# Regrouping TensorE's 512- and 256-column matmuls by width, and moving two operands by 32 bytes

## What is computed

```python
def conv_glu_ffn(x, norm_g, w_up, conv_w, conv_b, w_down):
    h = rms_norm(x, norm_g) @ w_up              # 1024 -> 2 * 2816
    c = conv_b + sum(conv_w[j] * shifted(h, j) for j in range(3))
    gate, up = jnp.split(c, 2, axis=-1)
    return x + (jax.nn.silu(gate) * up) @ w_down    # 2816 -> 1024

def swiglu_ffn(h, w13, w2):
    gate, up = jnp.split(h @ w13, 2, axis=-1)
    return (jax.nn.silu(gate) * up) @ w2

def reference(...):
    for layer in range(2):                      # phases L0 F0 L1 F1
        x = (diff_pool_layer, swa_layer)[layer](x, ...)
        x = conv_glu_ffn(x, ...)
    x = x + 0.5 * swiglu_ffn(rms_norm_2(x, g1), w13_1, w2_1)     # F2
    x = x + y @ w_out                           # y: conv module and attention of x (MIX)
    x = x + 0.5 * swiglu_ffn(rms_norm_2(x, g2), w13_2, w2_2)     # F3
    return rms_norm_2(x, final_norm)
```

## Time and profile before

| | |
|---|---|
| median of 3 runs | 1034.45 us (1033.99 to 1034.63) |
| the profiled execution | 1034.77 us |
| its span, first to last instruction | 1033.0 us |
| PE busy | 1008.0 us, 98% |
| PEld busy | 905.3 us, 88% |
| DVE / ACT / POOL busy | 746.7 / 625.5 / 354.9 us |
| mean granted TensorE clock | 0.998 |
| read from HBM | 181.4 MB, 177 GB/s over the span |

### The profile page before, as it was taken

One profiled execution on the slowest core, in us unless ns is written; L12 is line 12 of the kernel. 1 busy time (PEld: TensorE's weight loads), 2 busy tenths in 40 slices (PEclk: granted clock), 3 DMA queues, 4 the chain that ended last, 5 costly groups with the idle time before them and its releaser, 6 DMA issues.

```text
span 1033.0 us, 15900 instructions
## 1 busy us (share of the span) xinstructions
PE 1008.0 (98%) x6476; PEld 905.3 (88%) x6476; DVE 746.7 (72%) x1009; ACT 625.5 (61%) x880; POOL 354.9 (34%) x189
## 2 busy tenths in 40 slices
PE   7999999999998899999999999999999899999997
PEld 7889988888987798888888888888999698888886
DVE  5886999874577779998548765654799887666543
ACT  6776677663377477766436555544669866455531
POOL 1062176640000025675102545510148223555300
PEclk9999999999999999999999999999999999999999
DMA  9533575537441335656553755556342247555441
GB/s 351 207 135 123 214 270 209 201 131 257 146 163 42 125 142 209 239 188 207 180 200 123 247 202 175 191 204 220 123 155 95 83 172 259 180 204 186 141 163 41
DMA packets 27143, 183.45 MB, mean 178 GB/s; under 512 B 3008, under 2 KB 3136, under 8 KB 5824
## 3 DMA queue, kind: packets, MB, share of 16 engines
q1 hardware_dynamic: 26496, 181.40, 49.2%
q10 hardware_dynamic: 576, 1.05, 0.3%
HBM read 181.39 MB, written 1.05 MB: 177 GB/s over the span
## 4 chain that ended last, share of the span: by engine, by line
PE 85%; DVE 6%; ACT 5%; issue 2%; POOL 1%; DMA 0%; DVEq 0%; POOLq 0%; ACTq 0%
PE psum L335 85%; DVE wlo L1564 2%; ACT whi L1030 1%; POOL Y L2246 1%; ACT Pb L1165 1%; DVE Pb L1696 1%; DVE Pb L1567 1%; DVE QK L1570 0%; DVE QR L1564 0%; DMA gain_x<-in_x 0%; DVE bias L1570 0%; ACT Ob L1373 0%; ACT PT L1030 0%; ACT sq L1156 0%; DVE st L1567 0%
## 5 line engine op out<-in xcount | busy, mean ns | idle before, releaser
L335 PE MATMUL psum<-G,whi 128*128 128x512 f32 (+1 forms) x1856 | 551.3, 359 | 6.5 <-DVE wlo L1564 6.5
L1564 DVE TENSOR_TENSOR wlo<-raw,whi 128x2048 fp32r<-128x2048 f32 (+1 forms) x170 | 386.9, 2291 | 177.6 <-ACT whi L1030 177.5
L335 PE MATMUL psum<-G,wlo 128*128 128x256 f32 x1568 | 442.9, 282 | 0.0
L1030 ACT ACTIVATE whi<-raw 128x2048 fp32r<-128x2048 f32 (+1 forms) x170 | 315.9, 1869 | 148.0 <-PE psum L335 136.3
L335 PEld LDWEIGHTS psum<-G,whi 128*128 128x128 f32 x1856 | 330.6, 189 | 59.1 <-DVE G L1570 6.4
L335 PEld LDWEIGHTS psum<-G,wlo 128*128 128x128 f32 x1568 | 298.0, 190 | 0.1
L335 PE MATMUL psum<-A2room,whi 128*128 128x512 f32 (+1 forms) x784 | 228.6, 355 | 0.0
L2246 POOL TENSOR_TENSOR A2room<-Ab,A2room 128x512 fp32r<-128x512 f32 x44 | 146.8, 3337 | 127.6 <-ACT A2room L1030 127.6
L335 PE MATMUL psum<-A2room,wlo 128*128 128x256 f32 x656 | 184.9, 282 | 0.0
L335 PEld LDWEIGHTS psum<-A2room,whi 128*128 128x128 f32 x784 | 138.3, 188 | 20.6
L2246 POOL TENSOR_TENSOR Ab<-Cb 128x512 f32<-128x512 f32 x44 | 109.6, 2491 | 107.7 <-ACT Cb L1073 107.1
(11 more groups left out here) (192 smaller groups left out, 1034.7 us busy)
## 6 DMA issues: line engine op xcount, KB each, us to landing
raw<-in_wst SPq DMA_DIRECT2D x165, 1024.0 KB, 4.9
bias<-in_bias_c SPq DMA_DIRECT2D x1, 2048.0 KB, 9.3
raw<-in_wst SPq DMA_DIRECT2D x3, 512.0 KB, 8.0
raw<-in_wst ACTq DMA_DIRECT2D x4, 256.0 KB, 6.3
out<-bias SPq DMA_DIRECT2D x4, 256.0 KB, 2.1
gain_x<-in_x SPq DMA_DIRECT2D x3, 256.0 KB, 6.5
bias<-in_bias_a SPq DMA_DIRECT2D x1, 512.0 KB, 7.9
bias<-in_invcnt SPq DMA_DIRECT2D x1, 512.0 KB, 6.8
```

Of the source, the lines that this page charges most:

```text
L335: return pe.matmul(o, a, b, start=start, stop=stop, skip_group_check=True)
L1030: return act.activation(o, i, ACT.Copy)
L1564: return dve.tensor_tensor(o, a, b, op)
```

## The change

1. `wide` takes a list of tiles in place of a half, and issues for its two blocks of channels: all 512-column matmuls of the first block, all 256-column ones of the first, all 256-column ones of the second, all 512-column ones of the second. Most calls now cover the whole chunk (eight tiles); in F2 and F3 the first two chunks are still done in halves.
2. `down_wide` issues for an even bank two matmuls of 512 and then two of 256 columns, for an odd one two of 256 and then two of 512.
3. G2 is declared ahead of gain_x, so it starts at 128 modulo 256; gain_x does too, as before.
4. A2 starts at the beginning of its room in every phase, at 128 modulo 256. F3 keeps its place. Mhi and Mlo stay at 160.

```diff
+        G2 = sb("G2", [P, DT, 2, S], F32R)
         gain_x = sb("gain_x", [P, DT + DT * S])
         X = gain_x[:, DT:].rearrange("p (a b) -> p a b", a=DT)
-        G2 = sb("G2", [P, DT, 2, S], F32R)
...
-            A2 = A2room[:, 8:8 + FT * 2 * S].rearrange("p (t a s) -> p t a s", t=FT, a=2)
-            A2last = A2room[:, 0:FT * 2 * S].rearrange("p (t a s) -> p t a s", t=FT, a=2)
+            A2 = A2room[:, 0:FT * 2 * S].rearrange("p (t a s) -> p t a s", t=FT, a=2)
 
             def activations(ph):
-                a = A2last if ph == F3 else A2
-                return a[:, :, 0, :], a[:, :, 1, :]
+                return A2[:, :, 0, :], A2[:, :, 1, :]
...
-            def wide(b, i, h, ph=None, normed=None):
+            def wide(b, i, ks, ph=None, normed=None):
 
                 h3, l3 = weights(i, DT)
-                if h == 0:
+                if ks[0] == 0:
                     pe.wait_ge(s_lo, low_done(i))
-                for n in range(2):
-                    for k in range(4 * h, 4 * h + 4):
+
+                def highs(n):
+                    for k in ks:
                         if n == 0 and ph is not None:
                             pe.wait_ge(s_glo, 8 * ph + k + 1)
-                        if n == 0 and normed is not None:
+                        if n == 0 and normed is not None and k % 4 == 0:
                             pe.wait_ge(s_nlo, 2 * normed + k // 4 + 1)
-                        ws = slice(n * P, n * P + P)
-                        mm(bank[b + n], h3[:, k, ws], G2[:, k, :, :].rearrange("p a s -> p (a s)"), k == 0, False)
-                        last = mm(bank[b + n][:, 0:S], l3[:, k, ws], G2[:, k, 0, :], False, k == DT - 1)
-                if h == 1:
+                        last = mm(bank[b + n], h3[:, k, n * P:n * P + P], G2[:, k, :, :].rearrange("p a s -> p (a s)"),
+                                  k == 0 and n == 0, k == DT - 1 and n == 1)
+                    return last
+
+                def lows(n):
+                    for k in ks:
+                        mm(bank[b + n][:, 0:S], l3[:, k, n * P:n * P + P], G2[:, k, 0, :], k == 0 and n == 1,
+                           k == DT - 1 and n == 0)
+
+                highs(0)
+                lows(0)
+                lows(1)
+                last = highs(1)
+                if ks[-1] == DT - 1:
                     last.then_inc(s_used, 1)
...
-                    for kk in range(2):
-                        k = 2 * j + kk
-                        mm(o, h3[:, kk, ws], A2[:, k, :, :].rearrange("p a s -> p (a s)"), k == 0, False)
-                        done = mm(o[:, 0:S], l3[:, kk, ws], A2[:, k, 0, :], False, k == FT - 1)
+                    for high in ((True, False) if b % 2 == 0 else (False, True)):
+                        for kk in range(2):
+                            k = 2 * j + kk
+                            begin, end = k == 0 and high == (b % 2 == 0), k == FT - 1 and high == (b % 2 == 1)
+                            if high:
+                                done = mm(o, h3[:, kk, ws], A2[:, k, :, :].rearrange("p a s -> p (a s)"), begin, end)
+                            else:
+                                done = mm(o[:, 0:S], l3[:, kk, ws], A2[:, k, 0, :], begin, end)
...
-                        for h in range(2):
-                            wide(b, c0 + 2 * p + e, h, None, n if p == NARROW and e == 0 else None)
+                        wide(b, c0 + 2 * p + e, range(DT), None, n if p == NARROW and e == 0 else None)
...
-                    wide(at(ph, 4) + 2 * e, c0 + e, 0, ph if e == 0 else None)
+                    wide(at(ph, 4) + 2 * e, c0 + e, range(4), ph if e == 0 else None)
                 for e in range(2):
-                    wide(at(ph, 4) + 2 * e, c0 + e, 1, ph if e == 0 else None)
+                    wide(at(ph, 4) + 2 * e, c0 + e, range(4, DT), ph if e == 0 else None)
...
-                        wide(b + 2 * e, c0 + 2 * p + e, 0)
-                        wide(b + 2 * e, c0 + 2 * p + e, 1)
+                        wide(b + 2 * e, c0 + 2 * p + e, range(DT))
```

## The result

The changed kernel is slower: 1041.18 us median (1040.65 to 1041.71), against 1034.54 us for the kernel before in the same comparison; ratio 1.0065, 95% interval 1.0053 to 1.0078. The profiled execution took 1040.65 us with a span of 1038.9 us, 5.9 us more than before, so its trace holds nearly all of the difference. The forecast was 1029.2 us and the range 1024 to 1038; both missed.

What follows compares the result with a forecast made beforehand. TensorE, never waiting in wide stages, was taken as the bound. From the profiled 1034.77 us, regrouping took 5.25 and the move nothing, giving 1029.5; the median, 0.3 lower, was forecast at 1029.2 us, range 1024 to 1038.

Steps and rivals of the forecast that it cites:

- What bounds the kernel: Whole kernel: TensorE, busy 98%, waits for nobody in the seven wide stages; only distances between matmul starts count.
- What regrouping brings: Wide up and down projections: 3184 of 3616 width changes go, at 1.65 ns each, saving 5.25 us.
- price of a change of width: Wide stages: each switch between 512 and 256 columns costs 1.65 ns, from 346.7 against 343.4 ns a pair.
- The rule that spoke against it: Wide stages: the skill's gap, columns divided by clock plus 2.5 ns, makes regrouping worth 0 us.
- What the move brings: G2 and A2 moved 32 bytes to 128 modulo 256: 256-column matmuls assumed to stay at 116.6 ns, no gain or loss.
- slower rival: Both operands at 128 collide at 256 columns: wide lose 6.0 against 5.25 us gained, narrow up to 4.4; 1038 us, chance 0.18.
- the forecast's own test: F0's narrow stage, first A2room matmul to norm sum: 11.20 us if residue is neutral, 11.35 or more if it costs.
- narrow price: 1320 narrow matmuls with moving G or A2: up to 4.4 us lost, 1.3 if only 384 in A2room count.
- tokens-first chunks: 192 matmuls that also come to 128/128: could win 0.3 us, left out of the sum.
- Waits: Wide stages: no new wait costed; narrowest cover 0.25 us in F2's first half chunk; nothing added.
- No change: Rival: a low in a row costs 118.3 ns, or order is worth nothing; 1034.5 us, chance 0.15.
- more than forecast: Rival: same residue removes half the fixed 6.4 ns on 3128 matmuls, 10 us more; 1019 us, chance 0.13.

Runs made afterwards that it cites:

- order alone: The changed kernel with G2 and A2 put back at 160 modulo 256 (A2 of F3 at 128), regrouping kept; 1041.03 us, ratio to the kernel before 1.0061.
- two and two: F2's order, two highs then two lows, in a run of several orders with G2 64 bytes past the weights, edited from the changed kernel; 1031.78 us.
- grouped at 64: The changed kernel with wide moving operands 64 bytes past the weights and narrow inputs 32 past, grouped by width; 1032.56 us, ratio to the kernel before 0.9977.

## Why the prediction was wrong, point by point

**What bounds the kernel.** Right. PE waits for nobody in the wide stages after either, and all of the loss in the stage table's wide and narrow stages comes out of distances between matmuls.

**What regrouping brings.** This is the step that failed. It took 226.8 ns for highs from F3's down projection and 116.6 ns for lows from the narrow stages, and charged their difference to the alternation, 346.7 - 343.4 = 3.3 ns. But F3's row is at distance 0 and the narrow rows at distance 32. At 32 a high in a row takes 233.1 ns (order alone); at 0 a low takes 119.4 (changed kernel). No row of the trace of before shows both at one distance. F3's row has the weights moving besides: with the weights stationary, highs at distance 0 take 228.1 ns in runs of 16 and 232.5 in runs of four. The "price of a change of width" of 1.65 ns is not there where it could be tested: at distance 64 two and two is as fast as 16 and 16. In place of -5.25 us grouping at distance 32 brings +6.5. The prediction also called the narrow rows 116.6 "in two places, to 0.1 ns"; a third place in the same trace, F1's first narrow part, has 117.8. It named the risk in its last sentence, that no row shows a high in a row with weights stationary, but gave that risk no term and no rival.

**The rule that spoke against it.** The isolated gap of the Trainium skill ("TensorE: Matmul & The Clock Gate", section "Back-to-back issue gap") would make all of these runs equal in the wide stages. They span 344.8 to 353.4 ns a pair in the traces, so it does not serve for a choice of this size. The page gives it for an isolated matmul and says itself that in a stream weight loads have a share. The same page says in "Part 2: What happens when you issue a matmul" that the array reads the moving and the stationary operand through two independent ports. In the traces the pace still depends on how the two lie to each other: shifting both by 32 bytes changes nothing (1034.92 us), shifting one costs 12 us in the alternating order. Whether the ports have to do with it no run shows.

**What the move brings.** The mechanism of the slower rival holds where it said it would be seen: narrow matmuls went from 116.7 to 120.0 ns in F0, the upper bound of 119.9, not the 116.6 taken as likeliest. By the forecast's own test, 11.20 us or 11.35 and more in F0's narrow part, it is 11.52. The size is as that rival had it; that two streams get in each other's way is not shown. The choice rested on F3's 226.8 at 512 columns as the sign that 0 is harmless; with the weights stationary it is harmless neither at 256 columns nor, in runs of four, at 512 (232.5). Of the narrow price, 4.4 us at most, 2.5 us show in the narrow parts, L1 and MIX. The tokens-first chunks, left out as a possible gain of 0.3 us, lost: 118.3 ns before, 119.8 after.

**Waits.** Right: none came up. F2's first half chunk asks for its tiles earlier, and PE still doesn't wait.

**The rivals.** The slower one had the sign and, at 1038, the nearest time; measured 1041.2. Its narrow part, 1.3 to 4.4 us, holds (2.5). Its wide part was +0.75 us and is +3.9: it kept the highs at 226.8 and put the lows at 119.9, 346.7 a pair, where a down pair is 350.8, 2.2 us over 528 pairs, and an up pair 348.0, 1.7 us over 1280. It was given 0.18, and the range stopped at 1038 though its own upper end was 1039.5. "No change" (1034.5 us) and "more than forecast" (1019 us) fall with 1041.2.

## What to carry to other kernels

A pace read from one row holds for the width, the order and the relative place of both operands of that row; a sum of rows from different places is not a forecast. Where TensorE never waits, 8 or 16 floats of padding between two operands are worth trying: here the wrong place cost 1.2%, the best one found, with the order that goes with it, brought 0.2%. Order and padding have to be tried together, since each alone can lose where both together win: at distance 32 grouping loses, at 64 the alternating order does, and grouped at 64 is the fastest. Compare distances of starts over a whole stage; durations of single matmuls hide this.

## What the runs showed of the hardware that I had not expected

- The time from one float32r matmul's start to the next one's depends on how far the start of the moving operand lies past that of the stationary one (here taken modulo 256 bytes; no run tests the period), though not on that alone: 116.7 to 120.0 ns in the narrow stages, 226.8 to 233.9 for 512 columns in a row, with a mean granted clock of 0.995 to 0.999 in all of these runs. Moving everything by 32 bytes together changes nothing (1034.92 against 1034.77 us).
- The same instruction stream at the same distance can hold two paces over a whole stage: 353.3 and 346.7 ns a pair at distance 0. At distance 64 runs of lows take 117.5 and 113.8 ns in turn, and at 32 the narrow part of F1 goes from 117.8 to 116.7 ns at the norm sum. What chooses between them stays open.
- With weight loads of 64 columns in place of 128 an alternating stage took 353.3 ns a pair, more than the 346.7 of whole loads; with 32 columns it was 346.7 (one stage each, so that the columns did it is not shown).
